# Moving the jobs of the RWKV recurrence into another order on all five queues, with TensorE's waits on its products

## The reference

```
z = rms_norm(x) @ w_in                    # diff-attention q k v | rwkv r k v
o_diff = diff_attention(...)              # 4 heads, causal
kk = normalised(k * k_k);  k = k * (1 + (a - 1) * k_a)
for t in tokens:                          # 8 heads, state S of 64 x 64 each
    sa = S @ (-kk_t)
    S  = S * w_t + outer(sa, kk_t * a_t) + outer(v_t, k_t)
    y_t = S @ r_t
o_rwkv = (group_norm(y) + sum(r * k * r_k) * v) * g
x += concat(o_diff, o_rwkv) @ w_out;  x += moe(x);  x += per_layer_gate(x)
```

## Time and profile before

| | us |
|---|---|
| median of 3 runs (3240.16 to 3244.69) | 3241.17 |
| the profiled execution's own time | 3235.07 |
| its span, first to last instruction | 3233.4 |
| TensorE busy (91% of the span) | 2926.3 |
| VectorE busy (64%) | 2083.8 |
| ScalarE busy (50%) | 1607.4 |
| GpSimd busy (25%) | 801.9 |

### The profile page before, as it was taken

The page is one execution under the profiler, slowest core; times in us unless marked ns, Lnnn a source line. Parts: engine busy times, 40 slices in busy tenths (PEclk is TensorE's granted clock), DMA queues, the critical chain, the costliest instruction groups (busy, mean ns, idle before and its releaser), DMA issues. The chain is left out here.

```text
span 3233.4 us, 68007 instructions
## 1 busy us (share of the span) xinstructions
PE 2926.3 (91%) x24094; PEld 2385.2 (74%) x24094; DVE 2083.8 (64%) x3059; ACT 1607.4 (50%) x2651; POOL 801.9 (25%) x1076
## 2 busy tenths in 40 slices
PE   6999999997889895888888699989999999998899
PEld 5777887885566663776777588768888888887687
DVE  4444773224678774566666333479899999998675
ACT  3443211002777773444444211258888888887532
POOL 1000330001214125576766200111010001010353
PEclk9999999998999996999999799989999999999999
DMA  5555346656201001233333366556887966985663
GB/s 165 205 204 193 126 156 235 216 185 190 65 7 57 29 8 43 69 83 83 84 84 81 109 245 224 216 196 226 331 322 292 373 258 262 359 304 223 227 221 130
DMA packets 274054, 572.80 MB, mean 177 GB/s; under 512 B 51824, under 2 KB 87792, under 8 KB 265584
## 3 DMA queue, kind: packets, MB, share of 16 engines
q1 hardware_dynamic: 253152, 494.06, 44.3%
q0 software_dynamic: 11552, 41.95, 3.6%
q10 hardware_dynamic: 9072, 33.03, 2.5%
HBM read 418.42 MB, written 150.54 MB: 176 GB/s over the span
## 5 line engine op out<-in xcount | busy, mean ns | idle before, releaser
L627 PE MATMUL p_z<-w_in_part,hn_split 128*128 128x512 f32 x2304 | 536.9, 393 | 4.5 <-DVE w_in_part L431 4.5
L627 PEld LDWEIGHTS p_z<-w_in_part,hn_split 128*128 128x128 f32 x2304 | 434.2, 190 | 94.9 <-issue 4.9
L1890 DVE TENSOR_TENSOR e_w_part<-w_gate_up_sb,e_w_part 128x1024 fp32r<-128x1024 f32 x380 | 451.9, 1221 | 23.1 <-ACT e_w_part L1885 9.1
L1885 ACT CAST e_w_part<-w_gate_up_sb 128x1024 fp32r x380 | 398.2, 1052 | 120.5 <-PE pe_gate L2745 60.0
L2757 PE MATMUL pe_y<-e_w_part,e_hT 128*128 128x512 f32 x1128 | 271.8, 397 | 13.2 <-DVE e_w_part L1890 13.2
L2745 PE MATMUL pe_gate<-e_w_part,e_xT 128*128 128x512 f32 x1128 | 273.2, 398 | 6.5 <-DVE e_w_part L1890 6.5
L2745 PE MATMUL pe_up<-e_w_part,e_xT 128*128 128x512 f32 x1128 | 263.6, 389 | 0.0
L1890 DVE TENSOR_TENSOR e_w_part<-w_down_sb,e_w_part 128x1024 fp32r<-128x1024 f32 x188 | 218.0, 1221 | 58.7 <-ACT e_w_part L1885 58.4
L2757 PEld LDWEIGHTS pe_y<-e_w_part,e_hT 128*128 128x128 f32 x1128 | 210.8, 190 | 55.5 <-DVE e_w_part L1890 13.4
L2745 PEld LDWEIGHTS pe_gate<-e_w_part,e_xT 128*128 128x128 f32 x1128 | 210.9, 190 | 50.7 <-issue 7.1
L2745 PEld LDWEIGHTS pe_up<-e_w_part,e_xT 128*128 128x128 f32 x1128 | 211.7, 188 | 44.0
(11 more groups left out here) (459 smaller groups left out, 5578.8 us busy)
## 6 DMA issues: line engine op xcount, KB each, us to landing
w_gate_up_sb<-in_w_gate_dram SPq DMA_DIRECT2D x32, 2048.0 KB, 13.2
w_gate_up_sb<-in_w_up_dram SPq DMA_DIRECT2D x32, 2048.0 KB, 19.8
w_down_sb<-in_w_down_dram SPq DMA_DIRECT2D x32, 2048.0 KB, 9.4
hn_split<-s_hT SPq DMA_DIRECT2D x48, 1024.0 KB, 5.3
s_y<-e_y ACTq DMA_DIRECT2D x47, 512.0 KB
s_hT<-hn_split SPq DMA_DIRECT2D x16, 1024.0 KB, 6.4
s_y<-d_zeros SPq DMA_DIRECT2D x16, 1024.0 KB, 6.5
s_zn<-z_stage SPq DMA_DIRECT2D x48, 256.0 KB, 2.0
```

The lines of the kernel that those rows point to most:

```text
L627: last = nc.tensor.matmul(bank, hs[m % 3][:, a, k, :].bitcast(F32R), w_part(c, b)[:, k, :].bitcast(F32R), start=(k == 0 and a == b == 0), ...
L1885: return nc.scalar.copy(high, src)
L1890: return nc.vector.tensor_tensor(low, src, high, ALU.subtract)
```

## The change

The lists of all engines get a new order, and what follows from it is changed with them.

- TensorE: `cum` goes from the start of the step to the place behind `NN`, `NN` goes behind `TX2`, `Y` goes behind `X4`, `D` goes behind `TX4`, and `T0` to `T3` go together behind `X5`, ahead of `TX5`. `Tr4` is taken out of the ring of banks and uses the bank of `TX4a`.
- ScalarE: it takes the two copies of `NN` from VectorE. `sqk` goes to the start of the step, the decays' three operations behind `X3`, `vcopy` ahead of `Tr3`, and `TX5` behind `T3`.
- VectorE: `MR1` goes behind `TX2`, `S1` ahead of `kkn`, `Ah` ahead of `Y`, and `Bh` behind `TX4`. The scaling of `s2` comes to it from GpSimd.
- GpSimd: `ex` and `Rh` go behind `T_init`. `kk0` of the tile after next is made at the end of the step's preparation, and so the thirds of the loads that it needs get a semaphore of their own, `zk_in`. The two scalings on `c_tiny` go.
- SyncE: the loads hang on other jobs in the same order of loads. The decays' store goes behind four more loads.
- The increment in `ready` goes, and the waits stand ahead of the product itself.

```diff
-PE_JOBS = ["cum", "G3a", "G3b", "G1a", "G1b", "G2a", "G2b",
+PE_JOBS = ["G3a", "G3b", "G1a", "G1b", "G2a", "G2b",
            "Tr0", "X1a", "X1b", "Wa", "TX1a", "TX1b", "Wb",
-           "Tr1", "X2a", "X2b", "MR0", "MR1", "NN0", "NN1", "TX2a", "TX2b",
-           "Tr2", "X3a", "X3b", "S0", "TX3a", "TX3b", "Y0", "S1", "Ya", "Yb",
-           "Tr3", "X4a", "X4b", "TX4a", "TX4b", "T0",
-           "Tr4", "X5a", "X5b", "T1", "D", "TX5a", "TX5b", "T2", "T3"]
+           "Tr1", "X2a", "X2b", "MR0", "MR1", "TX2a", "TX2b", "NN0", "NN1", "cum",
+           "Tr2", "X3a", "X3b", "S0", "TX3a", "TX3b", "Y0", "S1",
+           "Tr3", "X4a", "X4b", "Ya", "Yb", "TX4a", "TX4b", "D",
+           "Tr4", "X5a", "X5b", "T0", "T1", "T2", "T3", "TX5a", "TX5b"]
...
-ACT_EV = ["Tr0", "X1a", "X1b", "Wa", "Wb", "Tr1", "P", "cumsb", "X2a", "X2b", "sqk", "Tr2", "X3a", "X3b", "Y0", "Pex",
-          "Tr3", "X4a", "X4b", "Tr4", "sqy", "T0", "T1", "TX5a", "TX5b", "T2", "T3", "vcopy", "D"]
-DVE_EV = ["G3a", "G3b", "G1a", "G1b", "G2a", "G2b", "TX1a", "TX1b", "kp", "MR0", "MR1", "TX2a", "TX2b", "NN0", "NN1", "ssk", "S0", "TX3a", "TX3b",
-          "bon", "kkn", "S1", "Ya", "Yb", "Bh", "Ah", "TX4a", "TX4b", "s1", "yc", "X5a", "X5b", "s2", "yn"]
-POOL_EV = ["kk0", "ex", "rkv", "Rh", "rk", "rsk", "T_init", "b", "Kh", "rsy", "bv", "out"]
+ACT_EV = ["sqk", "Tr0", "X1a", "X1b", "Wa", "Wb", "Tr1", "X2a", "X2b", "NN0", "NN1", "Tr2", "X3a", "X3b", "P", "cumsb", "Y0", "Pex", "vcopy",
+          "Tr3", "X4a", "X4b", "D", "Tr4", "sqy", "T0", "T1", "T2", "T3", "TX5a", "TX5b"]
+DVE_EV = ["G3a", "G3b", "G1a", "G1b", "G2a", "G2b", "TX1a", "TX1b", "kp", "MR0", "TX2a", "TX2b", "MR1", "ssk", "S0", "TX3a", "TX3b",
+          "bon", "S1", "kkn", "Ah", "Ya", "Yb", "TX4a", "TX4b", "Bh", "s1", "yc", "X5a", "X5b", "s2", "yn"]
+POOL_EV = ["rkv", "rk", "rsk", "T_init", "ex", "Rh", "b", "Kh", "kk0", "rsy", "bv", "out"]
...
+RING_JOBS = [n for n in MAIN_JOBS if n != "Tr4"]
+Z_IN, ZK_IN = 24 * 16, 8 * 16
...
 def bank_of(name):
-    return MAIN_JOBS.index(name) % BANKS if name in MAIN_JOBS else BANKS + PREP_JOBS.index(name) % 2
+    if name == "Tr4":
+        return bank_of("TX4a")
+    return RING_JOBS.index(name) % BANKS if name in RING_JOBS else BANKS + PREP_JOBS.index(name) % 2
...
-                sp.dma_start(dst[i % 2][p, cols], t[name][i * P + k * QUARTER:i * P + (k + 1) * QUARTER, cols]).then_inc(z_in[i % 2], 16)
+                sp.dma_start(dst[i % 2][p, cols], t[name][i * P + k * QUARTER:i * P + (k + 1) * QUARTER, cols]).then_inc((zk_in if c == 1 else z_in)[i % 2], 16)
...
                 ev("Kh", mul(Kh[n][:], kp[:], iP[:]))
+                if "next" in what:
+                    ...
+                        pool.wait_ge(zk_in[s], nth(i + 2, j, 2 - s) * ZK_IN)
+                    pool.tensor_tensor(rkv[s][:, k_], rkv[s][:, k_], z[s][:, k_], ALU.add)
+                    pool.drain()
+                ev("kk0", mul(kk0[:], rkv[s][:, k_], k_k[:]))
                 if "tail" in what:
                     pool.wait_ge(DV.sem, DV.value("s2", i))
-                    pool.tensor_tensor(tiny[:], s2[:], cst[:, 0, :], ALU.mult)
-                    pool.drain()
-                    pool.tensor_tensor(tiny[:], tiny[:], cst[:, 1, :], ALU.add)
-                    pool.drain()
-                ev("rsy", mul(rsy[:], tiny[:], cst[:, 2, :], ALU.pow))
+                ev("rsy", mul(rsy[:], s2[:], cst[:, 2, :], ALU.pow))
...
                             pe.wait_ge(e.sem, e.nth(n_, i + back))
-                    pe.sem_inc(passed, 1)
...
-                if "prep" in what:
-                    pe.wait_ge(z_in[n], nth(i + 1, j, 1) * 512 + 512)
-                job("cum", cum)
...
-                level(2); two_jobs(("MR0", "MR1"), mr, (AC, "Wb", 0)); two_jobs(("NN0", "NN1"), nn); filled(2)
-                level(3); s_(0); filled(3)
-                each("Y0", range(HV), y0); s_(1); two_jobs(("Ya", "Yb"), y_, (DV, "MR1", 0), (DV, "S0", 0))
-                level(4); filled(4); t_(0)
-                level(5); t_(1); chunked("D", range(HV), d_, (DV, "G2b", 0), (AC, "vcopy", 1)); filled(5); t_(2); t_(3)
+                level(2); two_jobs(("MR0", "MR1"), mr, (AC, "Wb", 0)); filled(2); two_jobs(("NN0", "NN1"), nn)
+                if "prep" in what:
+                    pe.wait_ge(z_in[n], nth(i + 1, j, 1) * Z_IN + Z_IN)
+                job("cum", cum)
+                level(3); s_(0); filled(3); each("Y0", range(HV), y0); s_(1)
+                level(4); two_jobs(("Ya", "Yb"), y_, (DV, "MR1", 0), (DV, "S0", 0)); filled(4)
+                chunked("D", range(HV), d_, (DV, "G2b", 0), (AC, "vcopy", 1))
+                level(5); t_(0); t_(1); t_(2); t_(3); filled(5)
```

More of the change, by code:

```diff
@@ L831, in _ @@
                     for i in range(2):
[L832 removed]
+                        sp.sem_inc(ahead["z_in"][i], Z_IN - 4 * 16)
             for s in spent:
@@ L1350, in _ @@
                     after(PO, "out", i - 1)
-                    for k, job in enumerate(("Ya", "Yb")):
+                    for k, job in enumerate(("Tr3", "X4a")):
                         after(PE, job, i)
                         store(i - 1, k)
-                    for k, job in enumerate(("Tr3", "X4a")):
+                    for k, job in enumerate(("X4b", "Ya")):
                         after(PE, job, i)
@@ L1359, in _ @@
                     load_ends(i + 1)
-                for k, job in enumerate(("X4b", "TX4a", "TX4b", "T0")):
+                for k, job in enumerate(("Yb", "TX4a", "TX4b", "D")):
                     after(PE, job, i)
@@ L1365, in _ @@
                 after(AC, "vcopy", i - 1)
-                for k, job in enumerate(("Tr4", "X5a", "X5b", "T1")):
+                for k, job in enumerate(("Tr4", "X5a", "X5b", "T0")):
                     after(PE, job, i)
@@ L1391, in ev @@
                 def ev(name, make):
-                    if group(name) in what:
+                    if ("next" if name == "kk0" else group(name)) in what:
                         PO.in_order(name)
@@ L1431, in step @@
                 if real:
+                    pool.wait_ge(AC.sem, AC.value("cumsb", i))
+                ev("ex", mul(cumsb[:], cumsb[:], sig[n][:], ALU.subtract))
+                ev("Rh", mul(Rh[:], rkv[n][:, r_], Pt[:]))
+                if real:
                     pool.wait_ge(DV.sem, DV.value("kkn", i))
@@ L1459, in step @@
                 ev("out", mul(yo[:], yo[:], g[n][:]))
-            steps(pool, step)
+            step(-1, 1, {"prep", "next"}, None)
+            step(0, 0, {"main", "prep", "next"}, None)
+            with pool.Fori(0, (TILES - 4) // 2) as j:
+                step(j * 2 + 1, 1, {"main", "tail", "prep", "next"}, j)
+                step(j * 2 + 2, 0, {"main", "tail", "prep", "next"}, j)
+            step(TILES - 3, 1, {"main", "tail", "prep", "next"}, None)
+            step(TILES - 2, 0, {"main", "tail", "prep"}, None)
+            step(TILES - 1, 1, {"main", "tail"}, None)
+            step(TILES, 0, {"tail"}, None)
         @block.scalar
@@ L1501, in turned, with narrow_copy @@
                     evac(f"TX5{f}", TT[s][:, half(f), :], narrow)
+                def narrow_copy(c):
+                    evac(f"NN{c}", NN[:, c, :, :], lambda b: b[:, 0:4 * DH].rearrange("p (a d) -> p a d", d=DH))
+                if "prep" in what and not (isinstance(i, int) and i < 0):
+                    act.wait_ge(PO.sem, PO.value("kk0", i - 1))
+                ev("sqk", lambda: nc.scalar.activation(sqk[:], kk0[:], ACT.Square))
                 tr(0)
@@ L1507, in step @@
                 tr(1)
+                x_(2, "a")
+                x_(2, "b")
+                narrow_copy(0)
+                narrow_copy(1)
+                tr(2)
+                x_(3, "a")
+                x_(3, "b")
                 if "prep" in what:
@@ L1517, in step @@
                 ev("cumsb", lambda: nc.scalar.copy(cumsb[:], bank("cum")))
-                x_(2, "a")
-                x_(2, "b")
-                ev("sqk", lambda: nc.scalar.activation(sq[:], kk0[:], ACT.Square), (PO, "kk0"))
-                tr(2)
-                x_(3, "a")
-                x_(3, "b")
                 evac("Y0", Y0[:])
                 ev("Pex", lambda: nc.scalar.activation(Pex[:], cumsb[:], ACT.Exp, scale=-DECAY), (PO, "ex"))
+                ev("vcopy", lambda: nc.scalar.copy(V[n][:], rkv[n][:, 2 * RW:3 * RW]), (PO, "rkv"), (PE, "Y0"))
                 tr(3)
@@ L1532, in step @@
                 t_(1)
+                t_(2)
+                t_(3)
                 turned("a")
                 turned("b")
-                t_(2)
-                t_(3)
-                ev("vcopy", lambda: nc.scalar.copy(V[n][:], rkv[n][:, 2 * RW:3 * RW]), (PO, "rkv"), (PE, "Y0"))
-                evac("D", AD[s][:, 1, :, :], heads)
             steps(act, step)
@@ L1651, in step @@
                     add_to_one(f)
-                ev("s2", lambda: nc.vector.tensor_reduce(s2[:], heads(sq[:]), AX.X, ALU.add), (AC, "sqy"))
+                if "tail" in what:
```

(4 more changed lines are left out.)

65 lines of the change are left out of this document (31 added, 34 removed).

## The result

The kernel after takes 3182.4 us (median of 4 runs, 3179.6 to 3186.88), the kernel before on the same chip 3240.66 us (median of 4, 3233.29 to 3244.69). The ratio is 0.9827, with a 95% interval of 0.9811 to 0.9844: 58 us less. The profiled execution took 3181.84 us, with a span of 3180.2 us, against 3235.1 and 3233.4 before.

The account below looks back on a forecast made before the run. No engine is full: the step is a chain that TensorE follows, with pauses. Terms of 2.3 us a step over 15 steps (35 us) plus 1 us took 3235.1 to 3199 profiled, median 3205 us; range 3165 to 3243.

Parts of the forecast that it names:

- rival A: TensorE's instruction fetch: its pauses, 2.2 us a step, go as well; 4.5 us a step in all, 3172 us; chance 0.15.
- `cum` leaves the start: TensorE's start of step: the pause ahead of `cum` goes and `G3`'s wait is covered; gain 1.1 us, bounds 0.5 and 1.14.
- `cum` and `NN` between `TX2` and `Tr2`: TensorE at level two: `cum` runs while VectorE fills `T`, covering the transposes' wait; gain 1.08 us a step, bounds 0.6 and 1.1.
- `Y` between `X4` and `TX4`: TensorE at level four: `Y`'s products fill the pause ahead of `TX4`; gain 0.3 us a step, bounds -0.3 and 0.9.
- `T0` to `T3` together: TensorE: small waits go, +0.1 us a step; `T2` waits for the copy of `T0`, -0.6, bounds 0 and -1.3.
- The waits on the products: TensorE's queue: 43 semaphore instructions of 51 ns go, about six places a step count; gain 0.3 us, bounds 0 and 2.2.
- The instruction fetch: TensorE's pauses at packet edges: present price of 2.2 us a step kept, no gain; bounds +2.2 and -3.7.
- The sum: All terms of a recurrence step together: 2.3 us a step gained, over 15 steps 35 us.
- `T0` ahead of the first tile: Ahead of the first tile: TensorE's 14.59 us wait for `Ah`, no longer behind `Bh`, shrinks by 1 us.
- Rival B: GpSimd, `ex` to `Pex` and back: this circle takes over as bound; only 1.2 us a step gained, 3222 us; chance 0.08.
- Rivals C and D: C: more fetch pauses on TensorE, slower, 3262 us, chance 0.12. D: waits only move, nothing gained, 3241 us, chance 0.07.

## Why the prediction was right or wrong

The prediction said 3205 us, 3165 to 3243, and faster with a chance of 0.80. It came to 3182.4: faster, inside the range, below the forecast's own band (3185 to 3222), and 10 us from rival A's 3172. The way is right, but the number owes more to a term that the forecast had put at nothing, and to the clock, than to its own terms. By these, a step at a time:

- **`cum` leaves the start, +1.1:** the size is right, the reason isn't shown. The 14.8 us are gone, and `G3` doesn't wait in their place (idle 0.0). But `cum` put back at the start of the new order waits for nothing either.
- **`cum` and `NN` between `TX2` and `Tr2`, +1.08:** right at its place, mis-sized in the sum. The third transpose's wait went (12.3 us in 13 steps, now 0.0), but the fifth, which had waited 1.6, now waits 11.3, 0.79 us in the step shown. So the group went from 14.0 to 11.3 us, 0.2 a step, outside the bounds of 0.6 and 1.1, of which the lower was for what "could come back". The two runs that take one cover away show that either suffices for the third.
- **`Y` between `X4` and `TX4`, +0.3:** ScalarE's part of `TX`'s wait fell by 1.6 us, 0.1 a step, and with `Y` put back the step is as long, less idle time against a lower clock: nothing that shows, inside the bounds (-0.3 to 0.9).
- **`T0` to `T3` together, +0.1 and -0.6:** the mechanism (`T2` waits for the copy of `T0`) was right, the size wrong and outside its bounds: (26.3 - 1.7) / 13 = 1.9 us. The price was taken from a place where ScalarE was free. Here its queue had `sqy`, which waits for VectorE. The prediction named `sqy` and didn't follow what it waits for.
- **The waits on the products, +0.3:** in the old order alone 5.5 us in 13 steps, 0.4 a step. That is close to 0.3 by luck: there 31 us of pauses went, and most of it was lost again in waits and clock. The 51 ns weren't what counted.
- **The instruction fetch, 0:** this is the step that failed: "I keep the present price, since there is no row for another". The pauses fell from 34 to 3.7 us, 2.3 a step, as rival A said ("if it gets ahead in its stream because it no longer stops at semaphore instructions"). That they went with the increments is shown; the reason that A gives isn't. They had also been larger than the forecast counted, 2.6 us a step and not 2.2, at 28 of 78 edges and not at one of six. The Trainium skill ("Runtime: NRT & Kernel Launch", section "Instruction fetch mechanics") calls the crossing of a block mostly hidden. The runs agree where the stream has no increments (2.6 and 3.7 us in 13 steps, with 76 packets each), and not where it has them (24 to 34 us).
- **The sum:** by what the idle rows name, the data waits rose from 38 to 43 us in 13 steps, -0.4 a step, the fetch gave 2.3, and the busy time 1.4 (18.5 / 13, with a granted clock of 0.96 for 0.94 and shorter products, 224 ns for 236 at `X`). That makes 3.3. The 2.3 of the forecast had no term for the clock at all, and its data waits were to fall by about 2.
- **Around the 13 steps:** `T0` ahead of the first tile came 5.2 us earlier instead of 1 (1260.31 to 1255.14), its wait 4.3 us shorter (14.59 to 10.25). All that stands ahead of and behind the 13 steps, up to the output projection, gave 19.5 us (586.1 - 432.0 = 154.1 against 523.4 - 388.8 = 134.6).
- **Rival B**, a circle through GpSimd, was to show as `Pex` waiting for `ex`. In the kernel after that wait is 0.9 us in 13 steps, so B wasn't it. **Rivals C and D** didn't come: the 34 us of pauses with the increments back are as many as before, not more.

Not settled are the 10.4 us behind the recurrence. The rows are the stretch from the router's last transpose to the experts' first, before and after.

```profile
2111.70:2131.80 20.10, 15.71 (x97) 12.97 (x95) 12.99 (x31) 3.56 (x5) 4.27 (x4) 0.90 0.75 292
```

```profile
2049.80:2075.40 25.60, 20.66 (x97) 18.05 (x96) 14.38 (x34) 3.69 (x5) 2.75 (x4) 0.73 0.49 190
```

The stretch has 5.5 of them, at a lower clock and with less moved by DMA, and the experts have 4.0 more (869.3 to 873.3). From the start of the projection to the end of the span the profiled executions fall into two groups. Five took 1403.0 to 1405.0 us: the kernel before, both runs with increments in the new order, the old order without them, and `NN` moved back. The nine others took 1410.0 to 1414.8. In all nine TensorE stands 2.4 to 3.3 us ahead of the router's products `pr_ids`, for an instruction of VectorE's queue, and in the kernel after these 64 products then take 421 ns each instead of 275. In the five it waits there for 0.2 us or not at all. The nine also are those in which TensorE's stream is the shortest, 36259 or 36291 instructions ahead of the projection against 36307 and more. So the change may have moved something there by the length of the stream, but no run shows how, and the cause stays open. For the comparisons it means that 10 us between two of these kernels can come from behind the recurrence, and that the stretches tell more than the whole time.

## What to carry to other kernels

Count what stands in an engine's instruction stream between its products: instructions that only carry a wait or an increment can cost by the fetch what they don't cost by their own 51 ns: 30 us of pauses came and went with them here. Follow each wait through the queue of the engine that ends it, one step further than the operation named: the copy was 0.59 us, the operation queued ahead of it 2.2 us late. And read a change of order in idle time and in clock: one standstill of 2 us can cost more busy time behind it, and when waits move from place to place with the step unchanged, look for one start that keeps its distance from another engine's end, as `T0` kept 0.10 us from `Bh`.
